# Requesting two experts' second-layer matrices at the issue of the first gather

## What is computed

```python
expert = g_idx[:, None] * EXPERTS_PER_GROUP + top_i        # 2 of 32 experts for each token
...
def run_block(args):
    x_blk, e = args
    return (jax.nn.silu(x_blk @ w1[e]) * (x_blk @ w3[e])) @ w2[e]
...
out = jnp.zeros((n_tok + 1, d), yb.dtype).at[buf_tok].add(yb)[:n_tok]
```

## Time and profile before

| what | value |
|---|---|
| time, three executions | 1470.69, 1470.92, 1474.62 us |
| median | 1470.92 us |
| time of the profiled execution | 1472.18 us |
| its span | 1470.4 us |
| PE busy | 1325.5 us, 90% of the span |
| DVE / ACT / POOL busy | 36% / 28% / 27% |
| bytes moved by DMA | 302.52 MB, of which the queue of SP 286.99 MB |

### The profile page before, as it was taken

How to read it: one execution, slowest core, us unless ns; L and a number is a source line. 1 busy time by engine, 2 the same in 40 slices (tenths; PEclk the granted TensorE clock), 3 DMA queues, 4 the chain that set the end, 5 groups by cost and what they waited for, 6 DMA issues and landing times. The chain is left out here.

```text
span 1470.4 us, 16826 instructions
## 1 busy us (share of the span) xinstructions
PE 1325.5 (90%) x6354; PEld 889.8 (61%) x6354; DVE 536.5 (36%) x1077; ACT 418.4 (28%) x814; POOL 390.7 (27%) x373
## 2 busy tenths in 40 slices
PE   6999998999999899987777887748999998999899
PEld 5677775898768633332222232317888887887566
DVE  3649957340242511111111111128311425464662
ACT  5333366263421100000000000016222224344641
POOL 7644223168310112211111111000445430000320
PEclk9999999999999999999999999988999999999999
DMA  7231222244405799999999999974323222221100
GB/s 211 62 113 58 70 103 81 90 145 144 172 33 208 309 415 421 418 422 421 421 424 422 422 423 422 422 306 149 115 86 114 86 86 86 87 88 56 58 22 36
DMA packets 74131, 302.52 MB, mean 206 GB/s; under 512 B 10392, under 2 KB 10440, under 8 KB 53328
## 3 DMA queue, kind: packets, MB, share of 16 engines
q1 hardware_dynamic: 66576, 286.99, 49.7%
q0 software_dynamic: 7488, 14.60, 3.1%
HBM read 295.26 MB, written 14.68 MB: 211 GB/s over the span
## 5 line engine op out<-in xcount | busy, mean ns | idle before, releaser
L774 POOL TENSOR_TENSOR ring_rounded<-ring,ring_rounded 128x512 fp32r<-128x512 f32 x192 | 252.2, 1350 | 345.0 <-ACT ring_rounded L1526 345.0
L902 PE MATMUL bank<-HT_rounded,ring_rounded 128*128 128x512 f32 (+1 forms) x576 | 221.2, 384 | 3.8 <-DVE ring_rounded L2452 1.9
L904 PE MATMUL bank<-HT_rounded,ring_rounded 128*128 128x512 f32 (+1 forms) x576 | 217.6, 378 | 0.0
L903 PE MATMUL bank<-ring_rounded 128*128 128x512 f32 (+1 forms) x576 | 217.4, 378 | 0.0
L1229 PE MATMUL bank<-ring,B 128*64 128x512 f32 x704 | 160.7, 602 | 27.0 <-DMA ring<-in_w 26.2
L904 PE MATMUL bank<-ring_rounded 128*128 128x512 f32 x352 | 139.0, 395 | 0.0
L1526 ACT ACTIVATE ring_rounded<-ring 128x2048 fp32r<-128x2048 f32 x54 | 103.0, 1914 | 115.0 <-DMA ring<-in_w_in_a 56.1
L902 PEld LDWEIGHTS bank<-HT_rounded,ring_rounded 128*128 128x128 f32 x576 | 108.4, 188 | 30.7 <-issue 5.9
L2343 DVE TENSOR_TENSOR B<-bank,small 128x512 f32<-128x512 f32 x32 | 22.1, 692 | 284.9 <-PE bank L1219 284.9
L1229 PEld LDWEIGHTS bank<-ring,B 128*64 128x64 f32 x704 | 49.2, 137 | 121.6 <-issue 86.3
L904 PEld LDWEIGHTS bank<-HT_rounded,ring_rounded 128*128 128x128 f32 x576 | 108.4, 188 | 20.3
(11 more groups left out here) (400 smaller groups left out, 1992.4 us busy)
## 6 DMA issues: line engine op xcount, KB each, us to landing
ring<-in_w SPq DMA_DIRECT2D x88, 1024.0 KB, 30.7
A<-in_w SPq DMA_DIRECT2D x20, 2048.0 KB, 33.1
ring<-in_w SPq DMA_DIRECT2D x11, 2048.0 KB, 33.3
HT<-in_w SPq DMA_DIRECT2D x20, 1024.0 KB, 32.9
XN<-in_w SPq DMA_DIRECT2D x20, 1024.0 KB, 29.6
ring<-in_w_in_a SPq DMA_DIRECT2D x16, 1024.0 KB, 5.1
ring<-in_w_in SPq DMA_DIRECT2D x14, 1024.0 KB, 7.2
ring<-in_w_in_b SPq DMA_DIRECT2D x8, 1024.0 KB, 5.5
```

The costliest lines, as they stand in the source:

```text
L774: last = pool.tensor_tensor(r32(lo), lo, r32_read(quarter(g, True)[:, k, :]), ALU.subtract)
L902: pe.matmul(o, r32(a_hi), r32(b_hi), start=first, stop=False)
L903: pe.matmul(o, r32(a_hi), r32(b_lo), start=False, stop=False)
L904: return pe.matmul(o, r32(a_lo), r32(b_hi), start=False, stop=last)
```

## The change

SP no longer waits until the first gather has landed (`xg_loaded0`), but until POOL has issued it (`gather_issued`). POOL raises that semaphore with an instruction of its own, between the first gather and the second. The waits on `xn_stored` and `x_stored` stay.

```diff
@@ -657,7 +657,7 @@
             for dst, src, loaded in (third[0], third[2]):
                 sp.dma_start(dst, src).then_inc(loaded, 16)
             sp.wait_ge(sem("xn_stored"), 16 * 2 * NT)
-            sp.wait_ge(sem("xg_loaded0"), 16)
+            sp.wait_ge(sem("gather_issued"), 1)
             for dst, src, loaded in third[4:]:
                 sp.dma_start(dst, src).then_inc(loaded, 16)
             sp.wait_ge(sem("x_stored"), 16 * 2 * NT)
@@ -823,6 +823,8 @@
 
             for q in range(3):
                 gather_rows(q, at=tab_g[:, q:q + 1])
+                if q == 0:
+                    pool.nop().then_inc(sem("gather_issued"), 1)
             wait_emptied(pool, U["table",])
 
             def step_rows(e, n):
```

## The result

| | kernel before | changed kernel |
|---|---|---|
| median of 20 runs | 1472.09 us | 1474.77 us |
| lowest run | 1469.17 us | 1472.46 us |
| profiled execution: time, span | 1472.18, 1470.4 us | 1479.30, 1477.5 us |

The ratio is 1.0022, with an interval from 1.0013 to 1.0032: 3.2 us slower, 1.9 to 4.7 us. (One run of the kernel before, of 2636.66 us, is left out of the ratio. The two medians of the table are closer, 2.7 us; the ratio and its interval are used from here on.) Forecast were 1.1 us faster and a median of 1469.8 us in a range that ended at 1473.4. The number is under the 0.3% that I called indistinguishable, but with 20 runs each it is clear of zero, and it lies on the side of the second rival.

A forecast was written before the change was run, and what follows sets the result against it. Weight loads were taken to bound the kernel from 640 us on. Of a 2.6 us earlier issue, 1.1 us counted as gain, the gather's 1.0 us being covered: 1470.92 - 1.1 = 1469.8 us, range 1468.6 to 1473.4.

The forecast's parts named there:

- the second rival: First gather pays more than its cover, so PE starts late: slower, 1473.3 us at full price; 22 in 100.
- SP's issue at 506.2: SP's first weight matrix is issued at 506.2 instead of 508.79 us, 2.6 us earlier, after the first gather's instruction.
- the price: Extra landing time of the first gather with weights beside it: between 0 and 4.8 us, taken as 1.0.
- the cover: Before PE's first turning, fillers hide 1.35 us of delay in the first gather's landing.
- the lead: SP's queue runs 2.6 us earlier; at expert 5's request 1.3 us are kept, 1.3 lost; gain taken as 1.1.
- fourth rival: The change does nothing: POOL's signal comes late, or gain and loss cancel; 1470.9 us; 16 in 100.
- the loads decide from expert 5's piece on: In the expert loop, weight loads set the pace from 640 us on; idle DMA time before moves the end.
- a delay of PE passes to that piece: Beyond the cover, a later PE start delays expert 5's request and moves the end one for one.
- the matrices' own arrival decides nothing: Second layers of experts 2 and 3 are used in PE's load-free part; their earlier arrival is worth nothing by itself.
- third rival: Late first gather plus a fall of PE's clock, 1.7 us more, up to 3.4: 1475.0 to 1476.7 us; 5 in 100.

The follow-up runs named there:

- e1: Changed kernel, but a small copy on POOL behind the first gather raises the signal instead of the bare semaphore instruction; 0.9989, 1.6 us faster than the kernel before.
- e3: Changed kernel, but a copy on POOL behind the third gather raises the signal; 1.0004 against the kernel before.
- e4: Changed kernel, but expert 3's matrix, the second one, waits for the landed first gather again; 1.0016 against the kernel before, +2.4 us.
- e8: e1 plus three filler matmuls in PE's wait for the gated values of expert 0; 0.9989 against the kernel before.
- e10: Kernel before plus three filler matmuls in PE's wait for the gated values of expert 0; 0.9999.
- e12: e1 once more, on another chip; 0.9989 against the kernel before.
- e7: Kernel before with four filler matmuls instead of eight ahead of PE's first turning of rows; 0.9999.
- e2: Changed kernel, but the bare semaphore instruction stands behind the third gather instead of the first; 0.9987 against the kernel before.
- e6: Kernel before, but SP holds the two matrices until PE has read half of expert 0; 1.0029, 4.3 us slower.

## Why the prediction was wrong

**The step that failed: "I take SP's issue at 506.2".** It rested on the sentence that the new instruction stands between the first gather and the second, and so runs at that place in time. That is T+2.4, 1.2 us behind the gather's start; SP issued at T+1.1, 0.12 us ahead of it. The instruction ran at T+1.0, when POOL had not yet started the gather. I looked for its cost (0 to 0.31 us) and not for its moment. From this the whole sign follows: the weights went first. e1 differs from the change in that instruction alone, does what I had predicted of the change, and comes out 1.6 us faster, where the forecast was 1.1. That these two are close is partly luck: the price, the cover and the lead, below, were off or held in one profile only.

The rule was to be had: the Trainium skill, page "PSUM — Partial Sum Buffer", section "Engine vs sequencer instructions", says that a nop is a sequencer instruction, and that the sequencer waits for earlier instructions to be dispatched, not to be completed. Its example is a matmul and a nop on PE; POOL's semaphore row at 512.2 us, ahead of the gather's start at 512.43, agrees with it, here behind an indirect DMA's instruction. My fourth rival named the opposite error, a signal that comes too late.

**The price of the gather** was bounded at 0 to 4.8 us and chosen near 0: 4.5 and 5.1 us were paid in the two profiles of the change, at the upper end and beyond it, because the head start on which I chose the low end wasn't there. With it, in e1, the price is nil (3.2 us).

**The cover of 1.35 us** was a draw. In the profile before, the eight fillers ran at half clock and lasted until T+6.3. In e1, e3, e4, e8, e10 and e12 they took 3.69 us at full clock (granted clock 1.00 in the windows of e8 and e10, 0.50 before). Three of these then waited for the gather, 0.48 us in e3, 0.57 in e10, 0.32 in e12, so they had no cover at all. In such executions every microsecond of the gather's delay reaches PE, and the turning moves from T+4.9 (e3) to T+9.5, not by 3.0 but by 4.6 us. The second rival is the mechanism that happened, PE waiting for the gather, which the prediction also named as its sign of being wrong. Its full price, 2.35 us, lies within the measured 3.2 (1.9 to 4.7) and next to the 2.5 in T to landing; whether the missing cover adds to it is not shown.

**The lead of which 1.3 us are lost** was also one draw. It needs the late request of T+35.4, which had both the slow fillers and the fall of the clock in expert 1. In e3, e7 and e10 the request came 3 us earlier and its piece landed only 9.6 to 9.8 us after it, behind a backlog. e2 has the late request and shows the term as I had it, a landing after 5.3 us on a queue run dry; e1, e8 and e12 have the earlier one (6.7, 8.6 and 8.0 us to landing), and e8's windows show the loss at the start instead. That the size fits all four is luck: a lead of 2.4 us in issue is worth some 1.5 us in landing (e1, e2, e8, e12: T+40.0 to 40.5; before, e3, e7, e10: T+41.7 to 42.1).

**What held:** the loads decide from expert 5's piece on (396.1 to 397.5 us in every profile that shows it); a delay of PE passes to that piece once the queue is dry (landing T+44.2 and T+44.6 in the two profiles of the change); the matrices' own arrival decides nothing (in e6 they came 6.7 us late and the request did not move). The fallen clock of the third rival shows no added cost in the two profiles of the change: against the profile before, the fall came in expert 0 instead of expert 1, moved and not added. It was added in e4 alone.

Open: what keeps the gather's first packet back for 4.5 us once the weights have gone first. The packets say that it is not the completion alone; e4 says that 2048 KB ahead of it are as bad as 4096. POOL's own instruction takes 1.09 us in both cases and ends at 513.52 in the changed kernel, 3.4 us ahead of the first packet; no row shows what happens in between.

## What to carry to other kernels

On POOL, a bare semaphore instruction that stands behind an indirect DMA in the program did not say that the DMA had started. To order two queues by such a signal, let an instruction that the engine itself executes raise it, as e1's copy does, and check the order in the trace. A small transfer that PE waits for is to be let out before bulk loads, and little is enough: with 1.4 us between its start and theirs it landed after 3.2 us, with 1.2 us after 3.6 (e2), and with theirs 0.1 us ahead after 8.2. Nothing was run between 1.2 us ahead and 0.1 us behind. And a margin read from one profile (here 1.35 us of fillers at half clock) is a draw; look at how the same place reads in a second profile before resting a choice on it.

## What was not expected of the hardware

- The bare semaphore instruction on POOL's queue ran at 512.2 us, the gather ahead of it from 512.43; behind three gathers it still released SP before the second had started (508.27 against 508.44).
- The first gather's landing turns on a head start of little more than a microsecond: 3.2 to 3.4 us with the weights issued 1.4 us after its start, 3.6 with 1.2 us, and 8.2 to 8.8 us with the weights 0.1 us before it, whether 2048 or 4096 KB stand there (8.4 us with 2048).
- Behind the weights, the gather's first packet moved only 4.5 to 4.7 us after its start, against 1.6 to 2.0 us with the gather ahead.
- SP's issue of the second matrix took 1.68 and 2.15 us in the two profiles of the changed kernel, 0.43 before.
